# Feed-forward products of a float32 transformer kernel: three 256-column matmuls per weight block become one of 512 and one of 256 columns

## The reference

```python
# four plain ones (ffn1_0, ffn2_0, ffn1_1, ffn2_1); widths 1024 -> 2 x 2816 -> 1024
a, b = split(rms_norm(x) @ w_in)          # two halves, 2816 features each
x = x + 0.5 * ((silu(a) * b) @ w_out)
# two with a causal convolution of width 3 over the tokens (conv_0, conv_1)
a, b = split(conv3(rms_norm(x) @ w_up) + bias)
x = x + rms_norm((silu(a) * b) @ w_down)
```

## Time and profile before

| | us |
|---|---|
| median of three runs | 1832.31 (1828.08 to 1835.67) |
| span of the profiled execution | 1831.9 |
| TensorE matmul busy | 1700.7 |
| TensorE weight load busy | 1636.6 |
| VectorE busy | 1185.9 |
| ScalarE busy | 904.3 |

### The profile page before, as it was taken

One profiled execution on the slowest core, in us unless ns is written; L12 is line 12 of the kernel. 1 busy time (PEld: TensorE's weight loads), 2 busy tenths in 40 slices (PEclk: granted clock), 3 DMA queues, 4 the chain that ended last, 5 costly groups with the idle time before them and its releaser, 6 DMA issues.

```text
span 1831.9 us, 33959 instructions
## 1 busy us (share of the span) xinstructions
PE 1700.7 (93%) x13128; PEld 1636.6 (89%) x13128; DVE 1185.9 (65%) x1907; ACT 904.3 (49%) x1546; POOL 14.2 (1%) x20
## 2 busy tenths in 40 slices
PE   6999999899999999996899999878999989779997
PEld 5999997799999999975799999767999988679997
DVE  6555656576666666667666665767886576578764
ACT  5544453454445444454454454355665442356652
POOL 1000000000000000000000000000000000000000
PEclk9999999899999999998899999988999999989999
DMA  7554552255446554540255456204554543035442
GB/s 270 177 182 144 205 199 104 70 202 184 174 155 217 184 183 142 204 153 35 81 197 182 160 166 236 92 15 166 183 184 140 197 190 108 34 137 182 169 158 86
DMA packets 47358, 286.11 MB, mean 156 GB/s; under 512 B 5996, under 2 KB 6764, under 8 KB 23968
## 3 DMA queue, kind: packets, MB, share of 16 engines
q1 hardware_dynamic: 44640, 278.94, 43.5%
q10 hardware_dynamic: 2240, 5.19, 0.8%
q0 software_dynamic: 384, 0.68, 0.1%
HBM read 283.74 MB, written 1.05 MB: 155 GB/s over the span
## 4 chain that ended last, share of the span: by engine, by line
PE 84%; DVE 9%; ACT 4%; issue 2%; DMA 0%; ACTq 0%; DVEq 0%
PE ps_gemm L129 78%; DVE s_wlo L89 3%; ACT s_whi L80 1%; ACT s_work L839 1%; PE ps_gemm L828 1%; PE ps_sum L178 1%; PE ps_gemm L803 1%; DVE s_small L879 1%; DVE s_work L875 1%; PE ps_s L803 1%; PE ps_sum L828 1%; ACT s_work L848 1%; PE ps_sum L760 0%; DVE s_work L898 0%; PE ps_gemm L1161 0%
## 5 line engine op out<-in xcount | busy, mean ns | idle before, releaser
L89 DVE TENSOR_TENSOR s_wlo<-s_wraw,s_whi 128x1024 fp32r<-128x1024 f32 (+3 forms) x608 | 629.5, 1077 | 491.6 <-ACT s_whi L80 491.5
L80 ACT ACTIVATE s_whi<-s_wraw 128x1024 fp32r<-128x1024 f32 (+3 forms) x608 | 539.7, 935 | 445.3 <-PE ps_gemm L129 438.3
L129 PE MATMUL ps_gemm<-s_xhi,s_whi 128*128 128x256 f32 x2504 | 717.2, 286 | 13.4 <-DVE s_xlo L239 9.0
L129 PE MATMUL ps_gemm<-s_xlo,s_whi 128*128 128x256 f32 x2504 | 711.7, 284 | 0.0
L129 PE MATMUL ps_gemm<-s_xhi,s_wlo 128*128 128x256 f32 x2504 | 711.6, 284 | 0.0
L129 PEld LDWEIGHTS ps_gemm<-s_xhi,s_whi 128*128 128x128 f32 x2504 | 483.9, 193 | 18.1 <-issue 11.3
L129 PEld LDWEIGHTS ps_gemm<-s_xlo,s_whi 128*128 128x128 f32 x2504 | 484.0, 193 | 1.3 <-issue 1.0
L129 PEld LDWEIGHTS ps_gemm<-s_xhi,s_wlo 128*128 128x128 f32 x2504 | 483.9, 193 | 0.0
L129 PE MATMUL ps_gemm<-hid_hi,s_whi 128*128 128x256 f32 x1344 | 381.4, 284 | 12.4 <-DVE s_wlo L89 6.9
L129 PE MATMUL ps_gemm<-hid_hi,s_wlo 128*128 128x256 f32 x1344 | 381.3, 284 | 0.0
L129 PE MATMUL ps_gemm<-hid_lo,s_whi 128*128 128x256 f32 x1344 | 380.9, 283 | 0.0
(11 more groups left out here) (322 smaller groups left out, 1248.8 us busy)
## 6 DMA issues: line engine op xcount, KB each, us to landing
s_wraw<-in_stream_dram SPq DMA_DIRECT2D x178, 1024.0 KB, 4.8
s_wraw<-in_stream_dram SPq DMA_DIRECT2D x96, 704.0 KB, 4.1
s_wraw<-in_stream_dram SPq DMA_DIRECT2D x16, 768.0 KB, 4.3
s_wraw<-in_stream_dram SPq DMA_DIRECT2D x14, 512.0 KB, 3.3
s_room<-in_o_bias_dram ACTq DMA_DIRECT2D x1, 1536.0 KB, 10.3
s_room<-in_mem_dram SPq DMA_DIRECT2D x4, 256.0 KB, 5.0
s_x<-in_x_dram SPq DMA_DIRECT2D x1, 1024.0 KB, 6.1
s_room<-in_e_alibi_dram ACTq DMA_DIRECT2D x1, 1024.0 KB, 5.6
```

The lines of the kernel that those rows point to most:

```text
L80: c.act.activation(c.whi[:, slot, s], c.wraw[:, raw, s], ACT.Copy).then_inc(c.hi_ready, 1)
L89: last = c.dve.tensor_tensor(c.wlo[:, slot, s], c.wraw[:, raw, s], c.whi[:, slot, s].bitcast(F32), ALU.subtract)
L129: last = pe.matmul(out, a, b, start=start and i == 0, stop=stop and i == 2, skip_group_check=skip)
```

## The change

A weight block of the four plain up-projections (4 x 22 x 16 = 1408 blocks) and of all six down-projections (6 x 176 = 1056 blocks) is now multiplied by `mm_wide`: the high weights meet the high and the low activations in one matmul of 512 columns, whose halves land in the two halves of a bank; the low weights meet the high activations in one of 256, added to the first half. The halves are summed when the bank is evicted. So that one moving operand reaches both, the high and low activations lie in one tensor (two runs of 256 columns, 8 KB apart for x, 22 KB apart for the hidden activations). An up unit of a plain stage now fills two banks (`per = 2`). ScalarE copies the two second halves (512 columns) to SBUF, VectorE adds the first halves out of PSUM, and in the late-scaled stages multiplies by the inverse root afterwards, in SBUF. ffn1_0 takes the same path without that multiplication. A down result takes two VectorE instructions instead of one. The down loops are written out straight on all three engines. The convolution up-projections keep `mm3`.

```diff
+def mm_wide(pe, bank, w_hi, w_lo, x_both, x_hi, start, stop):
+
+    pe.matmul(bank.rearrange("p (a t) -> p a t", t=T), w_hi, x_both, start=start, stop=False)
+    return pe.matmul(bank[:, 0:T], w_lo, x_hi, start=False, stop=stop)
...
         if g >= 4:
-            pe.wait_ge(c.bank_free, g - 3 + step)
-        bank = c.ps_gemm[:, g % 4, :]
+            pe.wait_ge(c.bank_free, g + per - 4 + step * per)
+        banks = [c.ps_gemm[:, g % 4 + i, :] for i in range(per)]
...
+                    if wide:
+                        last = mm_wide(pe, banks[half], *w, c.x_both[:, :, k, :], c.xhi[:, k, :], k == 0, k == KD - 1)
...
+    for n in range(KD):
+        pe.wait_ge(c.bank_free, g0 + n - 3)
+        bank = c.ps_gemm[:, (g0 + n) % 4, :]
...
-                last = mm3(pe, bank, *block(c, u, i), c.hhi[:, s], c.hlo[:, s], k == 0, k == NF - 1)
+                last = mm_wide(pe, bank, *block(c, u, i), c.h_both[:, :, k, :], c.hhi[:, k * T:(k + 1) * T],
+                               k == 0, k == NF - 1)
...
+    def hidden(j, turn):
+
+        step = 0 if turn is None else turn * 4
+        split_hi(c, u0 + j + 2, None if turn is None else (turn, 4))
+        if j:
+            silu(j - 1, step)
+        act.wait_ge(c.unit_done, u0 + j + 1 + step)
+        if NF * cnt.ffn + j >= 2:
+            act.wait_ge(c.hid_ready, NF * cnt.ffn + j - 1 + step)
+        if conv is None:
+            b = (g0 + 2 * j) % 4
+            act.activation(c.cv[:, j % 2, :, :], c.ps_gemm[:, b:b + 2, T:2 * T], ACT.Copy).then_inc(c.rest_ready, 1)
...
+    def summed(j, turn):
+
+        step = 0 if turn is None else turn * 4
+        split_lo(c, u0 + j + 2, None if turn is None else (turn, 4))
+        if j:
+            gate(j - 1, step)
+        b = (g0 + 2 * j) % 4
+        v = c.cv[:, j % 2, :, :]
+        dve.wait_ge(c.rest_ready, NF * cnt.wide + j + 1 + step)
+        dve.tensor_tensor(v, c.ps_gemm[:, b:b + 2, 0:T], v, ALU.add).then_inc(c.bank_free, 2)
+        if j:
+            rest(j - 1, turn)
+        dve.wait_ge(c.bank_free, g0 + 2 * j + 2 + step * 2)
+        if late:
+            dve.tensor_tensor(v, v, c.inv[:, :].unsqueeze(1).to_broadcast([P, 2, T]), ALU.mult).then_inc(c.scaled_ready, 1)
+            dve.wait_ge(c.scaled_ready, NF * cnt.late + j + 1 + step)
...
         if conv is None:
-            ins = dve.scalar_tensor_tensor(c.x2[:, s], bank, 0.5, c.x2[:, s], ALU.mult, ALU.add)
+            dve_step(c, cnt, dve.scalar_tensor_tensor(c.x2[:, s], bank[:, 0:T], 0.5, c.x2[:, s], ALU.mult, ALU.add))
+            ins = dve.scalar_tensor_tensor(c.x2[:, s], bank[:, T:2 * T], 0.5, c.x2[:, s], ALU.mult, ALU.add)
         else:
-            ins = dve.tensor_copy(c.xn2[:, s], bank)
+            dve_step(c, cnt, dve.tensor_copy(c.xn2[:, s], bank[:, 0:T]))
+            ins = dve.tensor_tensor(c.xn2[:, s], c.xn2[:, s], bank[:, T:2 * T], ALU.add)
```

More of the change, by code:

```diff
@@ L136, in block, with first_products_pe @@
     return c.whi[:, u % SPLIT, s], c.wlo[:, u % SPLIT, s]
-def first_products_pe(c, cnt, bank, u, ready, late, tile_sums=False):
+def first_products_pe(c, cnt, banks, u, ready, late, tile_sums=False):
     for k in range(KD):
@@ L304, in ffn_pe @@
         up(j, None)
[L305 removed]
+    g0 += per * NF
     u0 += NF
[L308 to L312, removed]
+    for n in range(KD):
+        pe.wait_ge(c.bank_free, g0 + n - 3)
+        bank = c.ps_gemm[:, (g0 + n) % 4, :]
         for half in range(2):
             u = u0 + 2 * n + half
[L315 removed]
+            pe.wait_ge(c.lo_ready, u + 1)
             for i in range(NF // 2):
@@ L393, in convolved @@
         if j:
             rounded(j - 1, turn, step)
[L396 to L413, removed]
+    for j in range(4):
+        hidden(j, None)
@@ L414, in ffn_act @@
+    with act.Fori(0, NF // 4 - 1) as lap:
+        for j in range(4, 8):
+            hidden(j, lap)
+    for j in range(NF // 4 * 4, NF):
+        hidden(j, None)
+    silu(NF - 1, 0)
+    rounded(NF - 1, None, 0)
+    cnt.conv += conv is not None
+    cnt.late += late
     logs_act(c)
-    u0, g0 = u0 + NF, g0 + NF
-    def output(n, turn):
-        step = 0 if turn is None else turn * 2
+    u0, g0 = u0 + NF, g0 + (NF if conv is not None else 2 * NF)
+    for n in range(KD):
         for half in range(1 if n == KD - 1 else 2):
@@ L485, in convolved @@
         bank = c.ps_gemm[:, (g0 + j) % 4, :]
[L486 to L492, removed]
+        dve.wait_ge(c.tap_ready, 2 * m + 2 + step * 2)
+        for back in (1, 2):
             for side in range(2):
@@ L502, in convolved @@
         dve.wait_ge(c.bank_free, g0 + j + 1 + step)
[L504 to L525, removed]
+    def summed(j, turn):
[13 more added lines that the diff above has]
+            dve.wait_ge(c.scaled_ready, NF * cnt.late + j + 1 + step)
+    hidden = summed if conv is None else convolved
+    for j in range(4):
+        hidden(j, None)
+    with dve.Fori(0, NF // 4 - 1) as lap:
+        for j in range(4, 8):
+            hidden(j, lap)
+    for j in range(NF // 4 * 4, NF):
+        hidden(j, None)
+    gate(NF - 1, 0)
+    rest(NF - 1, None)
+    cnt.conv += conv is not None
+    cnt.late += late
+    cnt.wide += conv is None
+    u0, g0 = u0 + NF, g0 + (NF if conv is not None else 2 * NF)
+    for n in range(KD):
         for half in range(2 if n < KD - 1 else 1 if conv is None else 0):
@@ L654, in feature_tiles_pe @@
             if t == 0:
-                last = first_products_pe(c, cnt, bank, u, ready, late, tile_sums)
+                last = first_products_pe(c, cnt, [bank], u, ready, late, tile_sums)
             continue
@@ L2219, in __init__ @@
     def __init__(self):
-        self.split = self.out = self.norm = self.sq = self.xn = self.ffn = self.two = self.conv = self.post = 0
+        self.split = self.out = self.norm = self.sq = self.xn = self.ffn = self.late = self.wide = self.conv = self.post = 0
         self.hn = self.hi = self.job = self.turn = self.yh = self.mem = self.step = self.columns = 0
```

113 lines of the change are left out of this document (49 added, 64 removed).

## The result

The changed kernel takes 1824.73 us (median of 11 runs, 1818.59 to 1830.76) where the kernel before takes 1834.09 us (11 runs, 1828.08 to 1837.52). The ratio is 0.9950, with a 95% interval of 0.9933 to 0.9967: about 9 us faster, where 22.6 us were forecast.

The account below looks back on a forecast made before the run. TensorE's own pace was taken to bound the changed stages. 32.0 us saved in matmuls, less 1.2, 1.4, 3.7, 1.5, 0.6 and 1.0 us of waits and chains, left 22.6 us: 1809.5 us, range 1800 to 1826.

Parts of the forecast that it names:

- What bounds the kernel: TensorE's own pace sets the changed stages, apart from one wait at each change from up to down.
- The matmul term: All 2464 changed blocks go from 360 to 347 ns, one fixed term of 13 ns saved each: 32.0 us gained.
- My bounds of 333 and 360: Limits in ns per block: 360 if the wide matmul costs two, 333 if the narrow one's fixed term also vanishes.
- Eviction and the ring in steady state: Up stages: extra eviction instructions and the two-unit ring cost nothing; 4.5 of 5.55 us used, 1.0 us to spare.
- Start of the late-scaled stages: TensorE must wait at unit 2 for unit 0's eviction: 0.4 us, three times, 1.2 us lost.
- Start of ffn1_0: Unit 1 waits for the memory stage's last two copies, starting at 51.0 instead of 49.83: together 1.4 us lost.
- Up to down: Longer waits at the third down unit: 3.7 us in three late-scaled stages, 1.5 in ffn1_0, 0.6 in two convolution stages.
- Ends of the convolution stages: The uncovered chain of copy, square, sum and mean grows by 0.5 us in each of two stages: 1.0 us lost.
- The rival of the clock: Four new waits of 1.5 to 2.5 us each bring half clock, 2.6 us each: 10 us, 1820 us; chance 12%.
- The wide matmul as costly as two: A block stays at 360 ns and only the extra waits remain: 1838.5 us, slower; chance 7%.
- the ring as gate: In up stages the eviction chain takes 5.8 us, each of 88 units waits 0.25 us: 1831.5 us; chance 6%.
- the fixed term that stays: The 13 ns hang on columns or operand changes, about a fifth is saved, 6.4 us: 1835 us; chance 5%.

Follow-up runs that it names:

- e2: The changed kernel with the logarithm table loaded on ScalarE after, not before, the splits of the third and fourth down unit; 1813.84 us, ratio to before 0.9902.
- e3: The changed kernel with both table loads (Silu, logarithm) moved after the splits on ScalarE; 1807.76 us, ratio to before 0.9871.
- e9: e3 with the memory stage's last two results copied out before, not after, the low part of ffn1_0's second unit; 1806.52 us, ratio to before 0.9856.
- e4: The changed kernel with the wide matmul's moving operand in one run of 512 columns, nearly all low activations left out, timing only; 1826.82 us, one run.
- e1: The changed kernel with the Silu table loaded on ScalarE after, not before, the weight split of unit 2; 1822.41 us, ratio to before 0.9957.
- e5: The kernel before with the wide matmul in the down-projections alone, up-projections as before; 1828.53 us, ratio to before 0.9981.

## Why the prediction was wrong

The direction and most terms were right; the gain was less than half of the forecast, and the time lies 1.3 us inside the upper end of the range.

- **What bounds the kernel:** right. TensorE's own pace sets the changed stages before and after.
- **The matmul term, 32.0 us, was mis-sized.** The step that failed is "2464 x 13 ns": the sum took 227 and 120 ns, each measured in a stream of its own kind, as prices that add. In a mixed stream they add up (346.7) only in one of the paces it can take. Measured: 4.7 us in ffn1_0 (352 x 13.3), 2.6 us in each late-scaled up stage (32 blocks at 346.7, 320 at 353.3), 10.6 us in the downs (1056 x 10), in all 23 us: 9 us less than 32. My bounds of 333 and 360 held it; my own spread of 2 ns a block did not.
- **Eviction and the ring in steady state, nothing:** right. No unit after the third waited for a bank.
- **Start of the late-scaled stages, 1.2 us:** 0.8, 0.5 and 0.5 us of wait, right in kind, 0.6 us short in all. What I did not see is that a pause of half a microsecond can cost 2.1 us more in the pace of the whole stage behind it.
- **Start of ffn1_0, 1.4 us:** the wait went from 1.9 to 3.25 us, ended by the copy at the time forecast: right.
- **Up to down:** 2.4 us in the late-scaled stages (2.5 forecast), 1.5 in ffn1_0 (1.5), 2.1 in the convolution stages (2.2): right.
- **Ends of the convolution stages, 0.5 us each:** the wait of TensorE there grew from 1.42 to 1.88 us: right. The straight loops cost nothing visible.
- **The rival of the clock, given 12%, came true** in four places at 1.5 to 1.6 us each, 6.3 us. It was priced at 2.6 us each, from a stretch of 6.0 us at half clock; these last some 3.4 us each. The evidence that I held against it, waits of up to 1.8 us at full clock, said nothing on waits of 2.4 us. That these bring it is shown by e2, e3 and e9: with them cut to 1.0 us none of nine late-scaled down stages lost its clock, against seven of nine with them.
- **The wide matmul as costly as two, the ring as gate, the fixed term that stays:** none of them. e4 excludes a cost of the second run, and the fixed term that goes is 13.3 ns in the fast pace. The Trainium skill's 2.5 ns (TensorE: Matmul & The Clock Gate, Back-to-back issue gap), which the page gives for single matmuls and not for a stream with a weight load each, would have given 2.5 ns a block; the runs show 6.7 to 13.3. The Trainium skill's warning on non-contiguous patterns (Advanced Engine Details and Errata, PSUM Cachelines) did not show in an operand of two runs.

By these numbers the forecast of 22.6 us less 9 for the pace, 6.3 for the clock and 0.6 for the starts gives 6.7 us; the changed stages of the profile show 7.5. The whole profile shows 4.5, for the convolution ups' 4.1 us and the mixers' 7.2 come on top, and the median of 11 runs shows 9.4, with an interval of some 3 us each way. So the account is good to the microsecond for the changed stages and not for the total.

What stays open: what decides between 346.7 and 353.3 ns at a restart, why the downs are at 350.0 alone (the operand's two runs are not it), what besides the length of a wait brings the half clock, and why the kernels with moved work have a lower mean clock from run to run.

## What to carry to other kernels

Prices of instructions from streams of one kind are an estimate, not a sum, for a stream of two kinds: leave room for a pace some 2% off (353.3 against 346.7 ns), and read the pace from starts in every stage. A change that trades TensorE work for a longer eviction chain should be judged with the waits at the stage changes: here two table loads on ScalarE, moved behind the work that TensorE waits for, turned a gain of 0.5% into 1.3%. Before pricing a lengthened wait by its length alone, ask whether any trace shows the clock full behind a wait that long. And compare by stage where the untouched parts vary by more than the effect.

## What the runs showed of the hardware

- A stream of alternating 512- and 256-column matmuls has paces of 346.7 and 353.3 ns a pair on the same instructions; a pause of 0.2 to 0.8 us can switch between them, in both directions, and without a pause the pace stayed for some 115 us (units 2 to 21 of an up stage). The repeated pattern is 349, 350, 361 ns in the slow one.
- At the change from up to down, TensorE waits of 2.4 us were followed by five or six blocks wholly or partly at 1.2 GHz in 7 of 9 cases, waits of 1.5 us or less in none of 24 (changed kernel, e1 to e5, e9); at the start of ffn1_0 one wait of 3.2 us was not followed by any (e4); at 1.2 GHz the wide and the narrow matmul take 427 and 213 ns, exactly their columns, with no fixed term left.
